# Two-layer hybrid decoder trunk on one core: attention bias tables requested in two parts, and the outputs and head sums of the attention loop moved

## The reference

```python
def hybrid_mixer(u, ...):
    proj = u @ w_in                                   # q, k, v, r, a | q, k, v | s_u | gate logits
    y_gla  = gla_mixer(g_q, g_k, g_v, g_r, g_a, ...)  # chunked linear attention, 4 heads
    y_diff = diff_attention(d_q, d_k, d_v, ...)       # below
    y_s5   = s5_mixer(s_u, ...)                       # state space, GELU, then z = y @ w_glu + b
    gates = sigmoid(gate_logits)                      # three gates of 1024 columns
    merged = (gates[:, :, 0] * (y_gla @ w_branch[0]) + gates[:, :, 1] * (y_diff @ w_branch[1])
              + gates[:, :, 2] * (y_s5 @ w_branch[2]))
    return merged @ w_out

def diff_attention(q, k, v, lam_vecs, lam_init, norm_g, rel_bias):
    for blk in range(L // Q_BLOCK):                   # 4 blocks of 128 queries, 8 maps (2 per head)
        logits = jnp.einsum('bmqd,bmkd->bmqk', qm[:, :, s:e], km[:, :, :e])
        bias = rel_bias[t5_bucket(dist)].transpose(2, 0, 1)
        p = jax.nn.softmax(jnp.where(dist >= 0, logits + bias, -jnp.inf), axis=-1)
        a = p[:, :, 0] - lam * p[:, :, 1]
        outs.append(jnp.einsum('bhqk,bhkd->bhqd', a, vh[:, :, :e]))
    o = jnp.concatenate(outs, axis=2)
    o = o * lax.rsqrt(jnp.mean(o * o, axis=-1, keepdims=True) + EPS)
```

## Time and profile before

| | us |
|---|---|
| median of 3 runs (2730.94 to 2732.38) | 2732.19 |
| profiled execution, its own time | 2733.83 |
| its span | 2731.9 |
| TensorE busy (97% of the span) | 2654.0 |
| VectorE busy (51%) | 1396.2 |
| ScalarE busy (35%) | 963.1 |
| idle of TensorE ahead of scores (L1082), 2 times | 18.1 |
| idle of TensorE ahead of turned maps (L1091), 9 times | 10.3 |
| mean granted clock of TensorE, share of full speed | 0.979 |

### The profile page before, as it was taken

The page is one execution under the profiler, slowest core; times in us unless marked ns, Lnnn a source line. Parts: engine busy times, 40 slices in busy tenths (PEclk is TensorE's granted clock), DMA queues, the critical chain, the costliest instruction groups (busy, mean ns, idle before and its releaser), DMA issues.

```text
span 2731.9 us, 34428 instructions
## 1 busy us (share of the span) xinstructions
PE 2654.0 (97%) x12925; PEld 2210.4 (81%) x12925; DVE 1396.2 (51%) x2146; ACT 963.1 (35%) x1177; POOL 75.1 (3%) x64
## 2 busy tenths in 40 slices
PE   6999999999989999999999999999999899999998
PEld 5888888987866888888888888899878578888886
DVE  5777326755245558532277752386342545653322
ACT  3333224644245432222142221346332643322212
POOL 0000001200000000000000000031000000000000
PEclk7999999999999999999999999999999999999999
DMA  8675222222241236322247633222223212332321
GB/s 260 200 229 178 100 92 74 78 70 93 62 93 61 79 108 213 126 92 100 100 139 231 225 113 104 74 82 78 87 86 62 83 62 93 108 123 95 105 92 47
DMA packets 268426, 306.99 MB, mean 112 GB/s; under 512 B 17783, under 2 KB 245499, under 8 KB 268324
## 3 DMA queue, kind: packets, MB, share of 16 engines
q1 hardware_dynamic: 268172, 305.23, 35.2%
q10 hardware_dynamic: 152, 0.35, 0.0%
HBM read 303.44 MB, written 2.45 MB: 112 GB/s over the span
## 4 chain that ended last, share of the span: by engine, by line
PE 91%; DVE 3%; ACT 2%; DMA 2%; issue 1%; SPq 1%; ACTq 0%; DVEq 0%
PE bank L633 26%; PE bank L635 25%; PE bank L634 25%; DMA raw<-in_w_branch 1%; PE bank L898 1%; PE bank L647 1%; PE bank L899 1%; PE bank L900 1%; PE bank L765 1%; PE bank L1098 1%; PE bank L1215 1%; PE bank L1062 1%; PE bank L1082 1%; PE bank L964 1%; PE bank L980 1%
## 5 line engine op out<-in xcount | busy, mean ns | idle before, releaser
L1745 DVE TENSOR_TENSOR w_both_lo<-raw,w_both_hi 128x2048 fp32r<-128x2048 f32 x200 | 459.6, 2298 | 619.5 <-ACT w_both_hi L1278 618.8
L633 PE MATMUL bank<-u_hi,w_both_hi 128*128 128x512 f32 x1928 | 763.0, 396 | 5.3 <-DVE u_lo L1738 2.6
L635 PE MATMUL bank<-u_hi,w_both_lo 128*128 128x512 f32 x1928 | 753.1, 391 | 0.0
L634 PE MATMUL bank<-u_lo,w_both_hi 128*128 128x512 f32 x1928 | 752.3, 390 | 0.0
L1278 ACT ACTIVATE w_both_hi<-raw 128x2048 fp32r<-128x2048 f32 x200 | 380.4, 1902 | 731.4 <-PE bank L635 702.3
L633 PEld LDWEIGHTS bank<-u_hi,w_both_hi 128*128 128x128 f32 x1928 | 363.4, 188 | 89.0 <-issue 7.5
L635 PEld LDWEIGHTS bank<-u_hi,w_both_lo 128*128 128x128 f32 x1928 | 362.9, 188 | 77.7
L634 PEld LDWEIGHTS bank<-u_lo,w_both_hi 128*128 128x128 f32 x1928 | 363.5, 189 | 73.0
L633 PE MATMUL bank<-g_hi,w_both_hi 128*128 (+1 forms) x704 | 276.2, 392 | 0.0
L635 PE MATMUL bank<-g_hi,w_both_lo 128*128 (+1 forms) x704 | 274.0, 389 | 0.0
L634 PE MATMUL bank<-g_lo,w_both_hi 128*128 (+1 forms) x704 | 274.0, 389 | 0.0
(11 more groups left out here) (392 smaller groups left out, 3175.3 us busy)
## 6 DMA issues: line engine op xcount, KB each, us to landing
raw<-in_ffn_w_up SPq DMA_DIRECT2D x88, 1024.0 KB, 5.1
ada_w<-in_w_ada SPq DMA_DIRECT2D x64, 1024.0 KB, 5.0
raw<-in_w_in SPq DMA_DIRECT2D x52, 1024.0 KB, 5.2
raw<-in_ffn_w_down SPq DMA_DIRECT2D x44, 1024.0 KB, 4.8
raw<-in_w_branch SPq DMA_DIRECT2D x12, 1024.0 KB, 5.0
first_ada_w<-in_w_ada SPq DMA_DIRECT2D x8, 1024.0 KB, 12.2
raw<-in_w_out SPq DMA_DIRECT2D x8, 1024.0 KB, 4.9
raw<-in_s_w_glu SPq DMA_DIRECT2D x4, 1024.0 KB, 5.0
```

The costliest lines, as they stand in the source:

```text
L633: pe.matmul(dst, hi, rhi, start=first, stop=False)
L634: pe.matmul(dst, hi, rlo, start=False, stop=False)
L635: return pe.matmul(dst, lo, rhi, start=False, stop=last)
L1745: v.tensor_tensor(w_lo[s][:, :], raw[s][:, :], w_hi[s][:, :].bitcast(F32), SUB).then_inc(lo_split[s].sem, 1)
```

## The change

Four edits. The maps of head 0 (2 of 8) are requested ahead and the other 6 behind the chunk `gg2`, and `bg0` is requested ahead of both, before SP's wait for `o_ready`; VectorE waits for the first part before block 0 and for the second before the maximum of block 4. In blocks 4, 8 and 12 the output of the closed head comes behind the dense tile, on ScalarE its squares behind the sigmoid of a gate tile; the sums of the squares come one block later, and VectorE keeps them behind the mixing. The chunk `dq1` is split ahead of the decay's exponentials. The low parts of `ys` are each done one step behind the product that they need, rather than all four at the end.

```diff
--- before.py
+++ after.py
@@ -419,6 +419,7 @@
         o_normed = signal("o_normed", 8)
         yga_done = signal("yga_done", 4)
 
+        first_bias_loaded = signal("first_bias_loaded", 16 * P // BIAS_COPIES)
         bias_loaded = signal("bias_loaded", 16 * P // BIAS_COPIES)
         scores_ready = signal("scores_ready", 32)
 
@@ -602,16 +603,21 @@
                     load_chunk(L, name)
                 sp.wait_ge(out_ready.sem, out_ready.of(L, 4))
                 sp.dma_start(w_alpha[:, :], gla_w_alpha[L]).then_inc(alpha_loaded.sem, 16)
-                for name, _, _ in MIXER[17:25]:
+                for name, _, _ in MIXER[17:26]:
                     load_chunk(L, name)
+
+                def load_bias(begin, end, loaded):
+                    for a in range(P // BIAS_COPIES):
+                        lines = bass.AP(tensor=bias_copies.tensor, offset=P - 1 - BIAS_COPIES * a + begin * BIAS_COPIES * LINE,
+                                        ap=[[LINE - 1, BIAS_COPIES], [BIAS_COPIES * LINE, end - begin], [1, SEQ]])
+                        sp.dma_start(bias_tab[BIAS_COPIES * a:BIAS_COPIES * (a + 1), begin:end, :], lines).then_inc(loaded.sem, 16)
 
                 sp.wait_ge(o_ready.sem, o_ready.of(L, GLA_HEADS))
                 sp.wait_ge(line_stored, 32)
-                for a in range(P // BIAS_COPIES):
-                    lines = bass.AP(tensor=bias_copies.tensor, offset=P - 1 - BIAS_COPIES * a,
-                                    ap=[[LINE - 1, BIAS_COPIES], [BIAS_COPIES * LINE, N_MAPS], [1, SEQ]])
-                    sp.dma_start(bias_tab[BIAS_COPIES * a:BIAS_COPIES * (a + 1), :, :], lines).then_inc(bias_loaded.sem, 16)
-                for name, _, _ in MIXER[25:]:
+                load_bias(0, 2, first_bias_loaded)
+                load_chunk(L, MIXER[26][0])
+                load_bias(2, N_MAPS, bias_loaded)
+                for name, _, _ in MIXER[27:]:
                     load_chunk(L, name)
                 load_ffn(L, 1, L * CHUNKS + C_FFN2, ffn2_w_up, ffn2_w_down)
 
@@ -1166,11 +1172,11 @@
                     hd, qb = divmod(i, TB)
                     if i + 1 < DIFF_HEADS * TB:
                         diff_scores(L, *divmod(i + 1, TB))
-                    if hd and qb == 0:
-                        diff_out(L, hd - 1)
                     for name, k in BESIDE_DIFF[i]:
                         chunk_tile(L, name, k, (yga_hi, yga_lo, 4, YGA) if name[0] == "b" else None)
                     if hd and qb == 0:
+                        diff_out(L, hd - 1)
+                    if hd and qb == 1:
                         head_ms(L, 4 + hd - 1, 7)
                     diff_turn(L, hd, qb)
                 chunk_tile(L, "gd2", 0)
@@ -1619,6 +1625,7 @@
                 split_chunk(L, "bs1")
 
                 split_chunk(L, "dq0")
+                split_chunk(L, "dq1")
                 for t in range(2):
                     act.wait_ge(alpha_read.sem, alpha_read.of(L, t + 1))
                     st.did(act.activation(la[:, t, :], bank[4 + t][:, :], ACT.Abs, bias=vec(L, V_BALPHA + t, V_BALPHA + t + 1)))
@@ -1626,7 +1633,6 @@
                 st.did(act.activation(la[:, :, :], la[:, :, :], ACT.Exp, scale=-1.0))
                 st.wait()
                 act.activation(la[:, :, :], la[:, :, :], ACT.Ln, bias=1.0).then_inc(alpha_exps.sem, 1)
-                split_chunk(L, "dq1")
                 for t in range(2):
                     act.wait_ge(decay_sum.sem, decay_sum.of(L, t + 1))
                     act.activation(eb[:, t, :], lb[:, t, :], ACT.Exp, scale=1.0 / GLA_TAU).then_inc(gla_exps.sem, 1)
@@ -1674,11 +1680,11 @@
                         split_chunk(L, BESIDE_SPLIT[i])
                     if i + 1 < DIFF_HEADS * TB:
                         diff_exp(L, i + 1)
-                    if hd and qb == 0:
-                        head_squares(L, 4 + hd - 1, 7)
                     for name, k in BESIDE_DIFF[i]:
                         if name[0] == "g":
                             empty(L, name, k)
+                    if hd and qb == 0:
+                        head_squares(L, 4 + hd - 1, 7)
                     diff_copy(L, i)
                 split_chunk(L, "gd3")
                 empty(L, "gd2", 0)
@@ -2380,9 +2386,10 @@
                     v.wait_ge(emptied["act"].sem, emptied["act"].of(L, TILES["glu1", k].emptied))
                     stt(z_gate[:, k, :], b[:, :], vec(L, V_BGLU + k, V_BGLU + k + 1), z_gate[:, k, :], ADD, MUL)\
                         .then_inc(emptied["vec"].sem, 1)
+                    if k:
+                        split_tile(L, YS, k - 1, ys_lo, ys_hi, z_gate[:, k - 1, :])
                 v.wait_ge(emptied["vec"].sem, emptied["vec"].of(L, 4))
-                for k in range(4):
-                    split_tile(L, YS, k, ys_lo, ys_hi, z_gate[:, k, :])
+                split_tile(L, YS, 3, ys_lo, ys_hi, z_gate[:, 3, :])
                 split_chunk(L, "bs1")
                 for k in range(8):
                     b = tile_wait(L, f"bs{k // 4}", k % 4)
@@ -2459,18 +2466,20 @@
                     split_tile(L, YGA, k, yga_lo, yga_hi, gr[:, k, :])
                 split_chunk(L, "bg0")
 
-                v.wait_ge(bias_loaded.sem, bias_loaded.of(L, 16 * P // BIAS_COPIES))
+                v.wait_ge(first_bias_loaded.sem, first_bias_loaded.of(L, 16 * P // BIAS_COPIES))
                 diff_max(L, 0)
                 for i in range(DIFF_HEADS * TB):
                     hd, qb = divmod(i, TB)
                     for name, k in BESIDE_DIFF[i - 1] if i else ():
                         if name[0] == "b":
                             branch_tile(L, name, k, 4 * int(name[-1]) + k)
+                    if i + 1 == TB:
+                        v.wait_ge(bias_loaded.sem, bias_loaded.of(L, 16 * P // BIAS_COPIES))
                     if i + 1 < DIFF_HEADS * TB:
                         diff_max(L, i + 1)
-                    if hd and qb == 0:
+                    diff_mix(L, i)
+                    if hd and qb == 1:
                         head_keep(L, 4 + hd - 1, 7)
-                    diff_mix(L, i)
                     if i in BESIDE_SPLIT:
                         split_chunk(L, BESIDE_SPLIT[i])
                 split_chunk(L, "gd3")
```

## The result

The kernel after takes 2690.19 us (median of 4 runs, 2687.36 to 2694.30), the one before, in runs on the same chip, 2731.64 (2730.94 to 2732.38). The ratio is 0.985 (95% interval 0.9835 to 0.9864): 41.5 us faster, where 39 was forecast. The profiled execution of after took 2689.55 us, 44.3 less than that of before, and its span is 44.1 shorter.

The account below looks back on a forecast made before the run. TensorE, busy for 2654.0 of 2731.9 us, was taken as the bound. Gains of 18.8 − 2.1 + 17.4 + 2.8 + 2.4 = 39.3 us from 2733.83, less 1.6 to the median, gave 2693 us, range 2684 to 2708.

Parts of the forecast that it names:

- Tables and bg0: Ahead of the first scores in each layer: earlier bg0 shifts VectorE's chain by 10.1 and 8.65 us, gaining 18.8 us.
- Falls behind the new wait: Block 1, each layer: the new 2.8 us wait brings one clock fall in two, costing 2.1 us.
- Heads: Outputs, squares and sums at closed heads: 10.6 us of waits and 6.8 of clock, together 17.4 us gained.
- The residue of 0.25 a layer in block 9: Block 9, tiles of 12 matmuls: VectorE's work is tight there, so 0.25 us of wait stays in each layer.
- the clock term: Windows behind heads: most of 8.5 us lost to low clock returns, one fall kept, 6.8 us gained, bounds 0 and 8.5.
- ys and dq1: Waits for the low parts of ys and the split of dq1 shrink or go: 2.8 and 2.4 us gained.
- Rival (a): Gaps close but the clock stays low behind the new wait and the heads: 30.4 us gained, 2702; chance 0.18.
- Rival (b): VectorE bounds wherever tiles have 12 matmuls, so head gains return as waits for mixing: 21.9 gained, 2710; chance 0.08.
- (c): Ahead of the first scores, the first maximum still waits for late bg0 or tables: 22.6 gained, 2710; chance 0.06.
- (d): The clock falls at the 2.8 us wait and stays low through blocks 2 to 7: 47 slower, 2779; chance 0.02.

Follow-up runs that it names:

- bg0_behind_all: The changed kernel with bg0 requested behind both parts of the tables, as before the change: 2705.33 us.
- one_part: The changed kernel with the tables requested in one piece, as before, bg0 still ahead of them: 2691.63 us.
- filled_gap: The changed kernel with 12 matmuls of unused result put where TensorE waits ahead of the turned map of block 1: 2689.84 us.
- splits_only: The kernel before with only the low parts of ys and the split of dq1 moved: 2726.90 us.
- heads_only: The kernel before with only the head outputs, squares, sums and copies moved: 2713.06 us.
- mixing_first: The changed kernel with outputs, squares and head sums back in their old block and place, mixing still ahead of the copy of sums: 2704.05 us.
- tables_only: The kernel before with only the DMA edit, bg0 requested ahead and the tables in two parts: 2717.25 us.
- gg2_at_1: The changed kernel with VectorE's split of gg2 in block 1 instead of block 0: 2693.41 us.
- gg2_at_3: The changed kernel with VectorE's split of gg2 in block 3 instead of block 0: 2683.56 us.

## Why the prediction was right

The forecast, 2693 us for after, is 2.8 over the median, and against the profiled time of before the sum was 39.3 with 44.3 measured. By its steps:

- **Tables and bg0, 18.8.** From the first mark to the second turned map is 33.74 us before (804.01 − 770.27) and 23.66 after; in layer 1 32.26 and 23.66. Shift 10.08 and 8.60, 18.7 us in sum, as forecast. The forecast also said that the closed gap would become one of about 2.8 us in block 1; 2.65 was measured, in both layers. bg0_behind_all shows that the cause was the request of `bg0`; the cut, costed at nothing, gave and cost nothing (one_part).
- **Falls behind the new wait, −2.1.** Forecast as one fall in two at 2.1; two came, at 1.4 each (filled_gap): −2.8. The chance was too low: over the six kernels with this gap of 2.65 us, 11 of 12 were followed by a fall. The price was too high: it was the mean of 1.8 and 2.4 us read behind gaps of 9.8 and 8.3 us, and behind 2.65 us the low clock cost 1.6 us up to the end of the next tile, of which 0.2 would have been a wait for VectorE anyway. The two errors pull opposite ways and leave 0.7.
- **Heads, 17.4.** From the second turned map to the last mark the two layers took 118.42 + 115.67 = 234.1 us before, 215.4 after: 18.7 gained with both falls inside, 21.5 without them. Of the 234.1, 11.9 were idle, of the 215.4 0.2: 11.7, with 10.6 forecast. The residue of 0.25 a layer in block 9 didn't come. The other 9.8 are put down to the clock and narrow matmuls behind gaps, with 6.8 forecast and 8.5 as the upper bound. All falls behind heads went, where I had kept one, and some 1.3 us lie beyond the bound that the windows gave. How much the clock term was worth rests on the draw: it was read off one trace, with four falls in six. With splits_only, the same loop with two falls and without the wait of 1.57 us, the second turned map to the last mark took 228.2 us, so the gain without falls is 15.6 rather than 21.5. The forecast of 17.4 lies between, and so do the 18.7 of the medians of heads_only. That the term came out near was in part luck.
- **ys and dq1, 2.8 + 2.4.** Both waits are gone from the list, 5.7; the 0.25 us a layer that I left for `ys` didn't come.

The sum by measured terms: 18.7 − 2.8 + 21.5 + 5.7 = 43.1 against the trace of before, and 37.2 with 15.6 for the heads; the medians say 41.5. Rival (a), the clock that does not come back, was half right: the falls behind the new wait came in both layers, those behind heads went. Rival (b), VectorE as the bound in the later blocks, did not hold for after, but mixing_first shows how near it was: with the sums in the old block it is a wait of 2.0 us in just the block that the prediction called tight. (c) and (d) left no trace: no wait for `bg0` or the tables, and the clock was back within one window.

## What to carry to other kernels

A weight chunk requested behind a big table can hold up work that needs neither: look at what stands behind the waiting instruction on its engine, and put the small, early request first. When such a gap closes, compute what each engine meets next; here it was a split in front of a mixing, and moving it to where the following tile covers it brought 3.4 us more a layer, 1.4 of it clock. A small copy that waits for another engine belongs behind all the work that this other engine will soon wait for. And a stretch of one trace is a good measure only where the same work repeats to a few hundredths of a us; the old loop, with its short gaps, differed by 6 us between two traces.

## What the runs showed of the hardware

**Which gaps are followed by a low clock.** Over all traces of the loop, with the granted clock in the 5 us from the end of the gap: 0.70 us, none of 2; 1.43 us ahead of outputs, none of 10 at once; 1.1 us behind the narrow sums, 9 of 18 (0.50 or 0.66); 1.66 to 1.73 us, 2 of 4; 2.0 us, 2 of 2; 2.65 us, 11 of 12 (0.66 to 0.68); 7.3 to 9.8 us ahead of the scores, 8 of 8 (0.50 to 0.66). Seven other waits of 0.4 to 1.6 us ahead of turned maps were followed by none. Of the gaps of 1.1 us, those behind head 1, with the one of 1.43 us some 7 us ahead, were followed by a fall in 5 of 6 cases, those behind heads 0 and 2 in 4 of 12; no run takes the two gaps apart. The Trainium skill, "TensorE: Matmul & The Clock Gate", on the clock gate in Part 1, says that the window in which activity is looked at runs free of the kernel. The traces fit this: the gap of 2.65 us in tables_only, with the same work around it in both layers, was followed by 0.66 in layer 0 and 1.00 in layer 1.

**The clock elsewhere is drawn anew.** The rest, the program outside the two stretches, spans 2423.6 to 2432.8 us in the ten versions with all of the change's splits in it, though their programs hold the same work there. TensorE is busy there for 2382.2 to 2394.1 us and idle for 38.3 to 41.5, so most of the scatter is the clock. The low clock comes at the same places and differs in depth. Windows of gg2_at_1:

```profile
1360.00:1380.00 20.00, 19.10 (x89) 0.83 0.45 145
1740.00:1760.00 20.00, 20.00 (x112) 0.83 0.44 99
```

and of gg2_at_3:

```profile
1360.00:1380.00 20.00, 18.65 (x85) 1.00 0.33 106
1740.00:1760.00 20.00, 18.87 (x96) 0.91 0.58 145
```

(1 − 0.83) x 20 = 3.4 us twice against 0 and 1.8: 5 of the 9.2 us between these two are here. This is why a step of 3 us in the loop (filled_gap) could not be seen in the medians, and why the stretch was the better measure.
